# Decoder trunk with grouped experts: the two norms' weights are fetched as single-partition rows and spread by TensorE

## What is computed

```python
def layer_norm(x, g, b):
    mu = x.mean(-1, keepdims=True)
    var = jnp.square(x - mu).mean(-1, keepdims=True)
    return (x - mu) * lax.rsqrt(var + LN_EPS) * g + b

x = layer_norm(ALPHA * x + h, ln_mix_g, ln_mix_b)       # first norm
m = grouped_moe(x, router_w, w_gate_up, w_down)          # (silu(a) * b) @ w_dn per expert
x = layer_norm(ALPHA * x + m, ln_ffn_g, ln_ffn_b)       # second norm
```

## Time and profile before

| | |
|---|---|
| median of three runs | 890.27 us |
| profiled execution, its own time | 890.4 us |
| its span | 888.3 us |
| PE busy | 848.9 us (96%) |
| DVE busy | 407.7 us (46%) |
| ACT busy | 257.9 us (29%) |
| POOL busy | 61.1 us (7%) |
| moved by DMA | 260.16 MB, mean 293 GB/s |
| granted TensorE clock, mean | 0.986 |

### The profile page before, as it was taken

The page is one execution under the profiler, slowest core; times in us unless marked ns, Lnnn a source line. Parts: engine busy times, 40 slices in busy tenths (PEclk is TensorE's granted clock), DMA queues, the critical chain, the costliest instruction groups (busy, mean ns, idle before and its releaser), DMA issues.

```text
span 888.3 us, 16749 instructions
## 1 busy us (share of the span) xinstructions
PE 848.9 (96%) x7214; PEld 498.9 (56%) x7214; DVE 407.7 (46%) x661; ACT 257.9 (29%) x471; POOL 61.1 (7%) x72
## 2 busy tenths in 40 slices
PE   9999999999999999999896999999999999999886
PEld 7889788777888878733231464556433332333332
DVE  5588866777587574782221110121031411422237
ACT  6223435354358232430321011211220210211222
POOL 2200000000000000001000100000011001100103
PEclk9999999999999999999998999999999999999999
DMA  8922131313213259989999999999999999999992
GB/s 333 347 96 96 52 138 48 142 49 119 95 48 142 96 200 400 422 338 373 408 381 396 388 412 406 395 406 402 416 403 399 419 401 403 421 408 418 416 374 110
DMA packets 49465, 260.16 MB, mean 293 GB/s; under 512 B 5722, under 2 KB 6126, under 8 KB 24176
## 3 DMA queue, kind: packets, MB, share of 16 engines
q1 hardware_dynamic: 43184, 240.21, 68.5%
q0 software_dynamic: 6208, 18.89, 5.7%
HBM read 248.01 MB, written 13.42 MB: 294 GB/s over the span
## 4 chain that ended last, share of the span: by engine, by line
PE 79%; DMA 6%; DVE 5%; ACT 4%; SPq 3%; issue 2%; DVEq 0%; ACTq 0%
PE ps L1107 21%; PE ps L747 10%; PE ps L748 9%; PE ps L752 9%; PE ps L1130 9%; PE ps L1118 6%; DMA raw_e<-in_expert_w_gate_up 5%; PE ps L1154 4%; SPq L502 3%; PE ps L1168 1%; ACT sc L1410 1%; PE ps L1092 1%; PE ps L794 1%; PE ps L821 1%; ACT hi_m L1357 1%
## 5 line engine op out<-in xcount | busy, mean ns | idle before, releaser
L1107 PE MATMUL ps<-raw_e,xt_strip 128*32 128x512 f32 x1888 | 208.3, 595 | 7.6 <-DMA raw_e<-in_expert_w_gate_up 7.4
L1107 PEld LDWEIGHTS ps<-raw_e,xt_strip 128*32 128x32 f32 x1888 | 60.2, 110 | 146.7 <-issue 130.7
L2096 DVE TENSOR_TENSOR strip<-strip,ps 64x1536 f32<-64x1536 f32 (+2 forms) x18 | 24.2, 1343 | 216.9 <-ACT strip L1537 216.8
L747 PE MATMUL ps<-xh,hi_m 128*128 128x512 f32 x272 | 107.9, 397 | 0.0
L748 PE MATMUL ps<-xl,hi_m 128*128 128x512 f32 x272 | 106.2, 390 | 0.0
L1537 ACT ACTIVATE strip<-ps 64x1536 f32<-64x1536 f32 (+2 forms) x18 | 20.0, 1111 | 265.9 <-PE ps L1107 194.9
L1130 PE MATMUL ps<-raw_e,hT 128*32 128x512 f32 x752 | 86.7, 601 | 3.9 <-DMA raw_e<-in_expert_w_down 3.9
L1670 DVE SCALAR_TENSOR_TENSOR cacc<-hg,cwt,cacc 128x512 f32<-128x512 f32 x120 | 82.2, 747 | 0.0
L1638 DVE TENSOR_TENSOR lo_m<-raw_m,hi_m 128x2048 fp32r<-128x2048 f32 x27 | 61.9, 2291 | 43.0 <-ACT hi_m L1357 42.9
L1118 PE MATMUL ps<-raw_e,xt_strip 128*32 128x256 f32 x1280 | 73.1, 391 | 3.5 <-DMA raw_e<-in_expert_w_gate_up 3.5
L752 PE MATMUL ps<-xh,lo_m 128*128 128x512 f32 x272 | 67.2, 389 | 0.0
(11 more groups left out here) (321 smaller groups left out, 937.6 us busy)
## 6 DMA issues: line engine op xcount, KB each, us to landing
raw_e<-in_expert_w_gate_up SPq DMA_DIRECT2D x110, 1024.0 KB, 21.3
raw_e<-in_expert_w_down SPq DMA_DIRECT2D x60, 1024.0 KB, 21.1
raw_m<-in_w_in_chunks SPq DMA_DIRECT2D x20, 1024.0 KB, 4.9
raw_e<-in_expert_w_gate_up SPq DMA_DIRECT2D x32, 512.0 KB, 18.6
yd<-zeros POOLq DMA_DIRECT2D x8, 512.0 KB, 6.8
raw_m<-in_w_o SPq DMA_DIRECT2D x4, 1024.0 KB, 5.0
yt<-yd SPq DMA_DIRECT2D x4, 1024.0 KB, 17.9
raw_m<-in_w_conv_out SPq DMA_DIRECT2D x2, 1024.0 KB, 5.4
```

What stands on the lines that cost most here:

```text
L747: pe.matmul(dst, a1, b1, start=first, stop=False)
L1107: mm = pe.matmul(ps[at_, bank + g], xt[:, c, g * STRIP:(g + 1) * STRIP], cols[s], start=(c == 0), stop=(c == GU - 1))
```

## The change

The broadcasts from HBM go. POOL fetches the four vectors behind the scatter of place 1, each as one row of 4 KB onto one partition (0, 32, 64 and 96) of `norm_rows`. `spread(row, banks)` on PE multiplies a column of ones (one partition, 128 columns) by the row in two halves of 512, which puts the vector on all 128 partitions in two PSUM banks. The first norm's gain is spread ahead of the gates of step (5, 0), its shift ahead of those of place 6; DVE applies them from PSUM. The second norm's two vectors are spread behind the loop over late blocks; ACT copies them to `lnf`, and PE waits for that before both `add_residual` calls, which now stand behind `transpose_hidden`.

```diff
-        lnm = at("lnm", [P, D], F32, 112)
+        norm_rows = at("norm_rows", [P, D], F32, 148)
...
-            sp.wait_ge(chunk_used, nblk * 12 + LATE)
-            for j, v in enumerate((ln_ffn_g, ln_ffn_b)):
-                sp.dma_start(lnf[:, j], bass.AP(v.tensor, 0, [[0, P], [1, D]])).then_inc(lnf_in, 16)
             for t in range(PRESUM, NT):
                 read_back(t)
...
                 store_rows(slots[0:n, 3 * i + 1:3 * i + 2], ye[i % 2][0:n], y_out[i % 2])
                 if i == WIDE:
                     store_rows(slots[0:HALF, 3 * SECOND + 1:3 * SECOND + 2], ye2, second)
-                elif i == WIDE + 1:
-                    pool.wait_ge(second, 32)
-                    pool.dma_start(lnm, bass.AP(ln_mix_g.tensor, 0, [[0, P], [1, D]])).then_inc(ln_in, 16)
-                elif i == WIDE + 3:
-                    pool.wait_ge(ln1_gain, NT)
-                    pool.dma_start(lnm, bass.AP(ln_mix_b.tensor, 0, [[0, P], [1, D]])).then_inc(ln_in, 16)
+                elif i == 1:
+                    pool.wait_ge(chunk_used, LATER_AT + LATER)
+                    for row, v in enumerate((ln_mix_g, ln_mix_b, ln_ffn_g, ln_ffn_b)):
+                        pool.dma_start(norm_rows[row * STRIP:row * STRIP + 1], v).then_inc(ln_in, 16)
...
                 if isinstance(i, int) and i == WIDE:
+                    pe.wait_ge(x1_ready, NT)
                     pe.wait_ge(second, 16)
...
+            NORM_BANKS = (2, 5)
+
+            def spread(row, banks):
+
+                at_ = slice(row * STRIP, row * STRIP + 1)
+                for half, bank in enumerate(banks):
+                    mm = pe.matmul(ps[:, bank], ones[at_], norm_rows[at_, half * 512:(half + 1) * 512],
+                                   start=True, stop=True)
+                mm.then_inc(norm_bc, 1)
...
             for j in range(3, len(STEPS)):
+                if STEPS[j] == (WIDE - 2, 0):
+                    pe.wait_ge(ln_in, 64)
+                    pe.wait_ge(ye_ready, 2)
+                    pe.wait_ge(he_ready, 2)
+                    spread(0, NORM_BANKS)
+                elif STEPS[j] == (WIDE - 1, None):
+                    pe.wait_ge(ln1_gain, NT)
+                    spread(1, NORM_BANKS)
                 gate_up(j)
                 down(j - 1)
...
+            spread(2, (0, 1))
+            spread(3, (2, 5))
+            transpose_hidden(nblk - 1 + EXTRA, nblk - 1)
             pe.wait_ge(residual, NT)
+            pe.wait_ge(lnf_sb, 1)
             add_residual(PRESUM)
-            transpose_hidden(nblk - 1 + EXTRA, nblk - 1)
             add_residual(NT - 1)
...
+            act.wait_ge(norm_bc, 4)
+            act.activation(lnf[:, 0], ps[:, 0:2].rearrange("p a c -> p (a c)"), ACT.Copy)
+            act.activation(lnf[:, 1, 0:512], ps[:, 2], ACT.Copy)
+            act.activation(lnf[:, 1, 512:], ps[:, 5], ACT.Copy).then_inc(lnf_sb, 1)
             act.activation(warm, cst[:, 36:37], ACT.Sqrt)
...
             def gain():
 
-                dve.wait_ge(ln_in, 16)
+                dve.wait_ge(norm_bc, 1)
                 for t in range(NT):
-                    dve.tensor_tensor(x1[:, t], x1[:, t], lnm, ALU.mult).then_inc(ln1_gain, 1)
+                    for half, bank in enumerate((2, 5)):
+                        cols = x1[:, t, half * 512:(half + 1) * 512]
+                        ins = dve.tensor_tensor(cols, cols, ps[:, bank], ALU.mult)
+                    ins.then_inc(ln1_gain, 1)
...
                 if part != 0:
                     output(before)
-                if STEPS[j] == (WIDE + 3, None):
+                if STEPS[j] == (WIDE - 2, 0):
                     gain()
+                elif STEPS[j] == (WIDE - 2, 1):
+                    shift()
                 elif STEPS[j] == (WIDE + 5, None):
-                    shift()
                     gate_diagonals()
```

More of the change, by code:

```diff
@@ L413, in build @@
             sem(n) for n in ("diag_ready", "sum_ready", "fin_last", "presum"))
-        pool_set, lnf_in = sem("pool_set"), sem("lnf_in")
+        pool_set, norm_bc, lnf_sb = sem("pool_set"), sem("norm_bc"), sem("lnf_sb")
         idv, sel_blk, idx_mm = (sem(n) for n in ("idv", "sel_blk", "idx_mm"))
@@ L736, in _ @@
                 store_last(i - 1, (i - FIXED) * 2 + 2)
-            pool.wait_ge(lnf_in, 32)
+            pool.wait_ge(lnf_sb, 1)
             for t in range(NT - 1):
@@ L2137, in gain @@
             def gain():
-                dve.wait_ge(ln_in, 16)
+                dve.wait_ge(norm_bc, 1)
                 for t in range(NT):
-                    dve.tensor_tensor(x1[:, t], x1[:, t], lnm, ALU.mult).then_inc(ln1_gain, 1)
+                    for half, bank in enumerate((2, 5)):
+                        cols = x1[:, t, half * 512:(half + 1) * 512]
+                        ins = dve.tensor_tensor(cols, cols, ps[:, bank], ALU.mult)
+                    ins.then_inc(ln1_gain, 1)
             def shift():
-                dve.wait_ge(ln_in, 32)
+                dve.wait_ge(norm_bc, 2)
+                dve.wait_ge(ln1_gain, NT)
                 for t in range(NT):
-                    dve.tensor_tensor(x1[:, t], x1[:, t], lnm, ALU.add).then_inc(x1_ready, 1)
+                    for half, bank in enumerate((2, 5)):
+                        cols = x1[:, t, half * 512:(half + 1) * 512]
+                        ins = dve.tensor_tensor(cols, cols, ps[:, bank], ALU.add)
+                    ins.then_inc(x1_ready, 1)
                 for t in range(NT):
@@ L2152, in gate_diagonals @@
             def gate_diagonals():
-                dve.wait_ge(x1_ready, NT)
+                dve.wait_ge(second, 32)
                 for k in range(2):
@@ L2207, in _ @@
                                              ).then_inc(presum, 1)
-            dve.wait_ge(lnf_in, 32)
+            dve.wait_ge(lnf_sb, 1)
             for t in range(NT):
```

## The result

The changed kernel takes **893.21 us** (median of ten runs, 890.93 to 895.85), the kernel before, in ten runs beside them, 889.45 us (887.88 to 892.45). The ratio is 1.0037 with a 95% interval of 1.0024 to 1.0050: slower by 3.8 us between the medians. The forecast was 892.4 with a range of 889.0 to 894.7.

A forecast was written before the change was run, and what follows sets the result against it. PE and DMA are both full from 560 to 800 us; PE sets the pace, late transfers set the gates' end. 890.4 - 2.0 + 4.1 = 892.5, stated as 892.4 us against the median; 8-in-10 range 889.0 to 894.7.

The forecast's parts named there:

- E: End of PE's last gate chunk in the last block: 851.18 us in the kernel before, forecast at 849.2.
- -2.0 ahead of E and +4.1 behind it: Gates' end 2.0 us earlier; behind it, down chunks start 4.4 later, less a 0.36 wait: 4.1 us lost (3.7 to 4.6).
- the likeliest case: Whole kernel: the forecast of 892.4 us, within the 0.3% (2.7 us) measurable from no change; chance 0.50.
- the rival on the clock: Behind E: PE's granted clock falls before both residual sums, which with first down chunks pay 1.7 us: 894.1; chance 0.16.
- PE takes over from DMA: Last gates: the shift's spread moves PE's work by 1.91 us, so the eighth chunk starts at 847.2, after its transfer lands.
- as a rival: Ahead of E: transfers stay the bound, for instance if PE regains 1.7 us at 512.36; gain 2.5 to 4.3; chance 0.22.
- The transfers alone, 2.5 to 4.3: Ahead of E: without the first norm's two broadcasts the last gate chunk can land 2.5 to 4.3 us earlier.
- The spreads behind E, 3.3 taken, 2.9 "at best": Second norm's four spread matmuls on PE: 3.3 us, 2.9 with partial overlap; ACT's copies done at E + 5.7.
- one-row matmuls are cheap: Spreads at 0.27 us per matmul: +1.8 behind E, 2.5 to 4.3 gained before it, 887.9 to 889.7; chance 0.12.
- The two sums, 3.82 taken: Behind E, after the wait for `lnf_sb`: both `add_residual` calls take 3.82 us, down chunks start at E + 9.6.
- POOL: Four row issues, some 0.9 us each, delay the gather at 461.02 by 3.7 us, leaving 12.7 for landing; weight waits absorb lateness.
- DVE's work at its new places: DVE's gain from 512.7 (5.5 us) and shift from 538.3 (8.2 us) fall in idle stretches; nothing queues.

The follow-up runs named there:

- experiment 12: The changed kernel measured once more, unaltered, beside other runs: 893.8 us, ratio 1.0037 to the kernel before.
- experiment 1: Against the kernel before, only the first norm's vectors are spread; the second norm keeps its HBM broadcasts: 886.93 us, ratio 0.9969.
- experiment 2: Against the kernel before, only the second norm's vectors are spread; the first norm keeps its HBM broadcasts: 894.33 us, ratio 1.0045.
- experiment 3: The kernel before without the first norm's two broadcasts, nothing in their place on PE; DVE multiplies by 1 and adds 0: 886.9 us, ratio 0.9960.
- Experiment 10: The kernel of experiment 1 with the shift's spread issued three times ahead of place 6: 895.78 us, ratio 1.0074 to the kernel before.
- Experiment 6: The kernel before with the first residual sum moved behind the transposes, no vector spread: 893.47 us, ratio 1.0032.
- Experiment 4: The changed kernel plus seven full-depth 128x128 filling matmuls around the tail's transposes: 890.57 us, ratio 1.0004 to the kernel before.
- experiment 11: The kernel of experiment 1 with the two rows fetched behind the scatter of place 2 instead of 1: 887.98 us, ratio 0.9985 to the kernel before.
- experiment 5: The changed kernel with the second norm's spreads 32 rows deep, ACT's copies scaled by 1/32: 892.89 us, ratio 1.0035 to the kernel before.
- experiment 8: The kernel of experiment 7 with the second norm's spreads 32 rows deep: 891.57 us, ratio 1.0009 to the kernel before.
- experiment 9: The kernel of experiment 7 plus three full-depth filling matmuls between spreads and transposes: 889.48 us, ratio 1.0002 to the kernel before.
- experiment 7: The changed kernel with add_residual(NT - 1) ahead of the down chunks, add_residual(PRESUM) later, banks and copies reordered: 888.86 us, ratio 0.9988 to the kernel before.

## Why the prediction was right, and where it was off

**Sum and signs: right, in part by luck.** Forecast -2.0 ahead of E and +4.1 behind it; the change's first profile shows -2.1 and +5.0, its second (experiment 12) -3.5 and +4.0, and experiments 1 and 2 show both signs as measured times. The median is 0.8 us over the forecast. That is closer than the terms were: behind E the spreads with ACT's copies were forecast 1.7 us too long and the sums 2.4 too short, and the two errors nearly cancel. And the boundary of 0.3%, which the likeliest case was to stay within, was passed (slower, 0.37%), and what carried it over was the rival on the clock.

**"PE takes over from DMA": right within a microsecond, by another sum.** From the first gates of place 6 to the end of the last, 311 us of PE work stand in a row: 849.05 - 536.71 - 1.1 of waits = 311.2 after, 851.18 - 536.34 - 2.8 = 312.0 before (and 847.66 - 535.12 = 312.5 in experiment 12). In the change's profile the last two chunks still wait 0.54 and 0.55, against "no wait after 838"; in that of experiment 12 none does. PE and transfers are level there. The step that failed is the start: the forecast moved place 6 by 1.91, and it moved by 0.4, as PE got back 1.7 us at 512 when wait and low clock went. That was named, but as a rival. The size came out right since the waits did not vanish wholly.

**The transfers alone, 2.5 to 4.3:** experiment 3 measured 2.9. Right.

**The spreads behind E, 3.3 taken, 2.9 "at best": mis-sized.** Four matmuls took 1.98, what one pair takes. Both halves of the gain ran beside both halves of the shift, not only one of each. The Trainium skill (TensorE: Matmul & The Clock Gate, Part 3, Packing small matmuls) gives for matmuls on different row groups the duration of one and a few ns; reading that as 2.9 was my step, from the belief that the order of issue would part the pairs, and the trace speaks for the rule as it stands. ACT's copies were done at E + 4.0, not E + 5.7.

**The rival "one-row matmuls are cheap": refuted.** A pair of them took 1.98 us (534.80 to 536.71 and the like), as long as a pair 128 deep, where the rival had 0.5. Its bound was also worded wrongly: 1.13 us is the time of two matmuls, so 0.27 each is a quarter of it and not a half.

**The two sums, 3.82 taken: mis-sized, 6.20.** This ate what the spreads had spared, and more: E + 10.36, where the forecast had 9.6 and the rival on the clock 1.7 more. The rival's test ("PEclk is under 1 between E + 4 and E + 10") was met, 0.50 and 0.71. I had held against it that PE comes from full work. Experiment 12 refutes that in the change itself: behind 13.92 us of gates without a wait, the spreads and 0.73 and 0.81 us of idle time the clock was 0.66 from 852 to 856. Experiment 10 goes further, with one-row matmuls behind full work and no idle time at all. Experiment 6 shows a low clock behind 2.66 us of idle time alone, but its gates had waits, so it does not speak to this argument. Experiment 4 shows that the clock was worth about 2.9 us of the result. With the spreads' true length and the clock held the same sum gives E + 4.0 + 0.2 + 3.6, so +2.6 behind E and a net of half a microsecond, which is what experiment 4 measured (ratio 1.0004).

**POOL: the size right by luck.** The scatter and the gather next to each other before, then after, with the four issues between them:

```profile
459.76 0.96 POOL L665 DMA_INDIRECT yd<-ye,slots  x1 [16.38 <-DVE ye L2128]
```

```profile
461.47 0.97 POOL L662 DMA_INDIRECT yd<-ye,slots  x1 [15.99 <-DVE ye L2149]
462.40 0.60 POOL L685 DMA_DIRECT2D norm_rows<-in_ln_mix_g  x1
...
464.79 1.08 POOL L658 DMA_INDIRECT xe<-x1n,slots  x1 [0.30 <-issue]
```

The gather of the next tokens goes out 3.8 us later than before (461.02), near the forecast 3.7, but not for its reason. An issue costs 0.5, not 0.9: from scatter to gather POOL takes 3.3 us instead of 1.3, so the four rows delay it by 2.1. The other 1.7 lie ahead of the scatter, where only the execution differs (in experiment 12 it starts at 459.98). The tokens landed within the 12.7 us that were left, 12.5 after the issue, and their transposes start at 477.33, no later than the 477.46 of before. PE waited 3.12 us for them all the same, since its last gate chunk had come earlier; before, PE waited for that chunk:

```profile
475.60 1.94 PE L1107 MATMUL ps<-raw_e,xt_strip 128*32 128x512 f32 x8 [3.08 <-DMA raw_e<-in_expert_w_gate_up]
```

So the one wait took the other's place, and that waits for weights would absorb the delay was right (experiment 11).

**DVE's work at its new places** was free as argued: the gain's products end at 519.3, the shift's at 544.1, and DVE's next product starts at 551.76, with no wait of PE for `x1_ready`.

What stays open: why experiments 5, 8 and 9, with tails of 39.7 and 37.6 us in their profiles, are not faster. The stretch ahead of place 6 varies from run to run; the expert part itself starts between 375.4 and 379.1 us in the profiles of these kernels, and one profile each cannot part that from the edits.

## What to carry to other kernels

- Work that sits in a gap of the critical chain may be holding TensorE's clock: before moving it out, price what follows at half the clock, and if the gap must stay, fill it with short full-depth matmuls.
- Replace a broadcast transfer by a spread where both the transfer was waited for and PE's gap is real (the first norm here, -0.3%); where the transfer was free, as the second norm's was, the spread and the hand-over behind it can only cost.
- Two resources within 1 or 2 us of each other over 300 us of work give only the first of the savings on either one; take the better half of a change alone.

## What the runs showed of the hardware

- Depth matters to the granted clock, not only being busy. Experiment 10 has it at 0.50 over 8 us with PE busy throughout, behind full work; a single one-row pair in full work left it at 1.00. In the four profiles whose tail had one-row spreads and no filling matmuls (the change twice, experiments 2 and 7) it fell behind them, to between 0.50 and 0.66 in the lowest 4 us window; in two with 32-row spreads (5, 8) and two with filling matmuls (4, 9) it stayed at 1.00, with the same idle stretches or none. The Trainium skill (TensorE: Matmul & The Clock Gate, HAM oscillation) speaks of idle time between bursts, in its example of longer ones than the 0.7 and 0.8 us of the tail, so the prediction's "by that rule this case holds" said more than the section does; experiment 6 agrees with it, at 0.57 behind 2.66 us, but no idle time was needed in experiment 10. The same gap does not always have the same effect: behind 1.74 us at the same chunk the clock was 0.57 in the kernel before and 1.00 in experiment 2.
- Four fp32 matmuls of 1x512 on two row groups took 1.98 us, as long as two on one, though they are issued vector by vector.
- A row of 4 KB on POOL's queue costs 0.5 us of POOL. From the gather's issue to PE's start on its tokens, where PE waited for them, it took 11.2 us with two such rows ahead of it (experiments 1 and 2), 11.4 to 12.5 with four (the change twice, experiments 4 and 7), and 14.1 and 14.9 in experiments 5 and 8, with two of the four made into blocks of 128 KB.
